# Building one triangular inverse of a chunked scan from the other by 32x32 block transposes, with the projection beside it in half-width units

## The reference, cut to what matters

```python
def wkv_scan(r, v, decay, k, a_in, b_in, s0, reverse):
    """S_t = S diag(w_t) + (S a_t) b_t^T + v_t k_t^T, y_t = S_t r_t."""
    def step(S, inp):
        rt, vt, wt, kt, at, bt = inp
        sa = jnp.einsum('bhij,bhj->bhi', S, at)
        S = S * wt[:, :, None, :] + sa[..., None] * bt[:, :, None, :] + vt[..., None] * kt[:, :, None, :]
        return S, jnp.einsum('bhij,bhj->bhi', S, rt)
    ...
for d in range(2):
    y_c, s_ctx_end = wkv_scan(r_c, v_c, *dirs_c[d], zeros, reverse=(d == 1))
    y_l, _ = wkv_scan(r_l, v_l, *dirs_l[d], s_ctx_end, reverse=(d == 1))
...
g_na, g_pool, g_rw = split(sigmoid(merge_logits))     # merge_logits = h @ w_in[:, last 6144 columns]
```

## Time and profile before

| what | value |
|---|---|
| time, three runs | 3787.69, 3774.82, 3781.83 us; median 3781.83 us |
| profiled execution, first to last instruction | 3780.2 us |
| instructions in it | 60072 |
| TensorE busy, share of the span | 3524.4 us, 93% |
| VectorE, ScalarE, GpSimd busy | 54%, 18%, 15% |
| mean granted TensorE clock | 0.982 of full speed |
| mean DMA rate | 211 GB/s |
| scan stage, from its first to its last visit on TensorE | 2799.4 to 3438.5 us, 639.1 us |

### The profile page before, as it was taken

One profiled execution on the slowest core, in us unless ns is written; L12 is line 12 of the kernel. 1 busy time (PEld: TensorE's weight loads), 2 busy tenths in 40 slices (PEclk: granted clock), 3 DMA queues, 4 the chain that ended last, 5 costly groups with the idle time before them and its releaser, 6 DMA issues. The chain is left out here.

```text
span 3780.2 us, 60072 instructions
## 1 busy us (share of the span) xinstructions
PE 3524.4 (93%) x24875; PEld 1824.6 (48%) x24875; DVE 2048.1 (54%) x3270; ACT 698.6 (18%) x1383; POOL 563.2 (15%) x809
## 2 busy tenths in 40 slices
PE   6999998999989998999999999989998899888998
PEld 2354443334544445554444444543356676665443
DVE  1699983352356776557646566436533334344435
ACT  2100001122210111431100000335622222221000
POOL 0111111120000002000000110631113223332100
PEclk9999999999999999999999999999999999999999
DMA  9989995982244467335477686558854333335663
GB/s 366 333 302 330 344 347 208 330 326 77 73 183 175 175 239 263 106 126 202 166 257 255 227 326 229 167 190 273 266 158 152 107 104 112 105 100 181 240 223 111
DMA packets 362625, 799.01 MB, mean 211 GB/s; under 512 B 26630, under 2 KB 73790, under 8 KB 357746
## 3 DMA queue, kind: packets, MB, share of 16 engines
q1 hardware_dynamic: 259760, 459.54, 35.5%
q0 software_dynamic: 72992, 274.20, 20.1%
q10 hardware_dynamic: 29602, 61.42, 4.3%
HBM read 686.90 MB, written 108.18 MB: 210 GB/s over the span
## 5 line engine op out<-in xcount | busy, mean ns | idle before, releaser
L1228 PE MATMUL gemm_a_g_ps<-store_w,turned 128*128 128x512 f32 (+1 forms) x1152 | 457.6, 560 | 2.7 <-PEq L108 2.7
L759 DVE SCALAR_TENSOR_TENSOR pmods_acc<-pmods_w,cond,pmods_acc 128x512 f32<-128x512 f32 x540 | 384.4, 749 | 23.6 <-issue 0.5
L1228 PEld LDWEIGHTS gemm_a_g_ps<-store_w,turned 128*128 128x128 f32 x1152 | 209.4, 191 | 250.3 <-issue 250.3
L3084 PE MATMUL scan_g_ps<-store_w,turned 64*64 64x512 f32 x2048 | 288.1, 610 | 10.5 <-DVE outlet_stage L3098 6.8
L1228 PE MATMUL att_a_g_ps<-store_w,turned 128*128 128x512 f32 x512 | 240.2, 599 | 6.9 <-ACT outlet_stage L2812 4.2
L1228 PE MATMUL feat_g_ps<-store_w,turned 128*128 128x512 f32 x384 | 181.9, 622 | 14.6 <-ACT outlet_stage L2240 12.4
L1275 PE MATMUL out_c_g_ps<-store_w,turned 128*128 128x512 f32 x384 | 167.6, 592 | 0.0
L1228 PE MATMUL tail_g_ps<-store_w,tail_branch_t 128*128 128x512 f32 x384 | 165.7, 592 | 0.9 <-ACT tail_branch_t L3913 0.9
L3449 DVE TENSOR_TENSOR scan_tm<-scan_tm,scan_ps 128x256 f32<-128x256 f32 x128 | 53.8, 421 | 168.8 <-PE scan_ps L3337 168.6
L1228 PEld LDWEIGHTS att_a_g_ps<-store_w,turned 128*128 128x128 f32 x512 | 91.5, 191 | 100.0 <-issue 93.4
L3337 PE MATMUL scan_ps<-scan_tmt,scan_y 64*64 64x64 f32 x2560 | 118.9, 223 | 14.2 <-issue 10.7
(11 more groups left out here) (577 smaller groups left out, 5934.0 us busy)
## 6 DMA issues: line engine op xcount, KB each, us to landing
store_w<-in_w_in SPq DMA_DIRECT2D x160, 1024.0 KB, 7.9
pmods_w<-in_w_mod POOLq DMA_DIRECT2D x40, 2048.0 KB, 13.2
store_w<-in_a_w_in SPq DMA_DIRECT2D x48, 1024.0 KB, 10.9
store_w<-in_c_w_in SPq DMA_DIRECT2D x40, 1024.0 KB, 8.4
first_mods_w<-in_w_mod SPq DMA_DIRECT2D x32, 1024.0 KB, 14.3
store_w<-in_a_w_out SPq DMA_DIRECT2D x32, 1024.0 KB, 6.2
scan_raw<-s_feat SPq DMA_DIRECT2D x112, 256.0 KB, 4.5
s_feat<-feat_o POOLq DMA_DIRECT2D x16, 1536.0 KB, 7.9
```

What stands on the lines that cost most here:

```text
L759: v.scalar_tensor_tensor(a, src, x, a, ALU.mult, ALU.add)
L1228: mm = pe.matmul(to, lhs, self.store.slot[i % self.store.NS][:, k, :width], start=first, stop=last)
L3084: mm = pe.matmul(self.ps[r][halves[o], :], self.act_tile(k, tb)[halves[r], halves[o]], self.store.slot[i % self.store.NS][halves[r], k % 4 ...
```

## The change

- TensorE: `products` no longer forms `A_`; `level(k)` makes only one product, with `y1` and `tmt`, on the diagonal quadrants, for all five levels.
- VectorE: `y1` is made here (`y_`), as the product of `half` plus the identity, in place of ScalarE's copy. The product of `level` is then the new `tmt` itself. `turn` makes `tm` from it by three block transposes (even heads: 128 partitions; odd heads: two of 64 partitions, each to the other half of the partitions), then a drain. A new stage `t0` adds the identity to the first `tmt` and turns it. `tm` is wanted only up to blocks of 32, so a transpose of 32x32 blocks is a whole one.
- ScalarE: `tt{k}` copies the product of `level` to `tmt`; for levels 1 to 4 it waits until VectorE has turned it.
- GpSimd: the two additions of the identity go.
- The projection: the 14 inner contraction steps of a tile are issued as two halves of 256 columns with a `yield` after each; the first and the last step stay whole and count as two units, of which one is empty for each. There are now 512 units, 40 ahead of the first visit, and the room is 6 behind `products`, 4 behind `av`, 1 behind each `half` and each `level`, 2 behind others.

```diff
 class Stream:
+    PER_TILE = 2 * KD
@@ units
-                for r, o in ((0, 0), (1, 1), (0, 1), (1, 0)):
-                    mm = pe.matmul(self.ps[r][halves[o], :], self.act_tile(k, tb)[halves[r], halves[o]],
-                                   self.store.slot[i % self.store.NS][halves[r], k % 4, :], start=(k == 0), stop=(k == KD - 1))
+                for ch in [slice(0, NCH)] if k in (0, KD - 1) else [slice(0, NCH // 2), slice(NCH // 2, NCH)]:
+                    for r, o in ((0, 0), (1, 1), (0, 1), (1, 0)):
+                        mm = pe.matmul(self.ps[r][halves[o], ch], self.act_tile(k, tb)[halves[r], halves[o]],
+                                       self.store.slot[i % self.store.NS][halves[r], k % 4, ch], start=(k == 0), stop=(k == KD - 1))
+                    if ch.start == 0:
+                        yield
@@ rwkv_scan
-        n_units, lead = len(gemm_side.tiles) * KD, 20
-        share = {"products": 6, "av": 3, "half": 1}
+        n_units, lead = len(gemm_side.tiles) * Stream.PER_TILE, 40
+        share = {"products": 6, "av": 4, "half": 1, "level": 1}
@@ products
                 inner(d, AT, 1, 0)
-                inner(d, A_, 0, 1, cross=True)
@@ half(k)
-                    if k > 1:
-                        after(pe, d, "dve", g, s, f"t{k - 1}")
-                    elif lat:
-                        after(pe, d, "dve", g, s, "rk")
+                    after(pe, d, "dve", g, s, "rk" if lat and k == 1 else f"t{k - 1}")
@@ level(k)
-                    after(pe, d, "act", g, s, f"half{k}")
-                    if k > 1:
-                        after(pe, d, "dve", g, s, f"tt{k - 1}")
-                    ...
+                    after(pe, d, "dve", g, s, f"y{k}")
+                    after(pe, d, "act", g, s, f"tt{k - 1}" if k > 1 else "av")
+                    for h in range(HG):
                         for c in chunks:
+                            mm = pe.matmul(quarter(d, 2, 1)[c, h, :], y1[d][c, h, :], tmt[d][c, h, :], start=True, stop=True)
@@ vector
-                v.tensor_tensor(by_parity(tm[d]), a, mask_by_parity(d, FIRST_T), ALU.mult)
+            def turn(d, src):
+                even, odd = by_parity(tm[d])[:, 0, :, :], by_parity(tm[d])[:, 1, :, :]
+                v.transpose(even, by_parity(src)[:, 0, :, :])
+                for c in range(2):
+                    v.transpose(odd[chunks[1 - c]], by_parity(src)[chunks[c], 1, :, :])
+                v.drain()
+                v.sem_inc(dve_done[d], 1)
+            def t0(d, g, s, lat):
+                v.tensor_tensor(tmt[d][:, :, :], tmt[d][:, :, :], eye, ALU.add)
+                v.drain()
+                turn(d, tmt[d][:, :, :])
+            def y_(k):
+                def f(d, g, s, lat):
+                    after(v, d, "pe", g, s, f"half{k}")
+                    v.tensor_tensor(by_parity(y1[d]), crossed(d, 0, 1), by_parity(eye), ALU.add).then_inc(dve_done[d], 1)
             def t_(k):
                 def f(d, g, s, lat):
                     after(v, d, "pe", g, s, f"level{k}")
-                    v.tensor_tensor(by_parity(tm[d]), by_parity(tm[d]), crossed(d, 0, 0), ALU.add).then_inc(dve_done[d], 1)
+                    turn(d, quarter(d, 2, 1))
-            def tt_(k):
-                ...
-                order = [("ft", 0), ("ft", 1), ("at", 0), ("ak", 0), ("at", 1), ("ak", 1)]
+                order = [("ft", 0), ("ft", 1), ("at", 0), ("ak", 0), ("at", 1), ("ak", 1), ("t0", 0), ("t0", 1)]
@@ scalar
-                run[f"half{k}"] = copies(f"half{k}", lambda d, lat, x: [(by_parity(y1[d]), crossed(d, 0, 1))])
+                run[f"tt{k}"] = copies(f"level{k}", lambda d, lat, x: [(tmt[d][:, :, :], quarter(d, 2, 1))], f"t{k}" if k < N_LEVELS else None)
@@ gpsimd
-                    pool.tensor_tensor(tm[d][:, :, :], tm[d][:, :, :], eye, ALU.add)
-                    pool.tensor_tensor(tmt[d][:, :, :], tmt[d][:, :, :], eye, ALU.add).then_inc(pool_done[d], 1)
```

More of the change, by code:

```diff
@@ L3065, in load_after @@
             old, part = (end - self.store.NS - begin) // 4, (end - self.store.NS - begin) % 4
-            if old >= 0 and 2 * KD * old + KD + 4 * (part + 1) > n_units:
+            if old >= 0 and self.PER_TILE * (2 * old + 1) + self.PER_TILE // 4 * (part + 1) > n_units:
                 break
@@ L3155, in stages @@
                 + ["tz", "outer", "chain1"] + ["y"] * lat + ["chain2"],
-                "dve": ["ft", "at", "ak"] + ["rk"] * lat + [f"{a}{k}" for k in levels for a in ("t", "tt")][:-2] + [f"tt{N_LEVELS}"] + ["pm", "m1", "m2"],
-                "act": ["ft", "av"] + [f"half{k}" for k in levels] + ["tz", "outer"] + ["y"] * lat,
-                "pool": ["eye"] + [f"lt{k}" for k in levels] + ["dg"],
+                "dve": ["ft", "at", "ak", "t0"] + ["rk"] * lat + [f"{a}{k}" for k in levels for a in ("y", "t")][:-1]
+                + ["pm", "m1", "m2"],
+                "act": ["ft", "av"] + [f"tt{k}" for k in levels] + ["tz", "outer"] + ["y"] * lat,
+                "pool": [f"lt{k}" for k in levels] + ["dg"],
             }[eng]
@@ L3265, in turned, with inner @@
                 mm.then_inc(pe_done[d], 1)
-            def inner(d, o, x, y, cross=False):
+            def inner(d, o, x, y):
                 for hp in range(0, HG, 2):
                     for h, to in ((hp, 0), (hp + 1, 1), (hp, 1), (hp + 1, 0)):
-                        c = 1 - to if cross and h % 2 else to
-                        mm = pe.matmul(product(d, o)[chunks[to], h % 2, h // 2, :], head(ft[d], h, x)[:, chunks[c]],
-                                       head(ft[d], h, y)[:, chunks[c]], start=True, stop=True)
+                        mm = pe.matmul(product(d, o)[chunks[to], h % 2, h // 2, :], head(ft[d], h, x)[:, chunks[to]],
+                                       head(ft[d], h, y)[:, chunks[to]], start=True, stop=True)
                 return mm
@@ L3352, in tz_ @@
             def tz_(d, g, s, lat):
-                after(pe, d, "dve", g, s, f"tt{N_LEVELS}")
+                after(pe, d, "act", g, s, f"tt{N_LEVELS}")
                 for h in range(HG):
@@ L3417, in _ @@
             v.wait_ge(tables, 64)
+            eye = eye2[:, :].unsqueeze(1).broadcast_to([P, HG, HD])
             def ft_(d, g, s, lat):
@@ L3448, in f @@
                     after(v, d, "pe", g, s, f"level{k}")
-                    v.tensor_tensor(by_parity(tm[d]), by_parity(tm[d]), crossed(d, 0, 0), ALU.add).then_inc(dve_done[d], 1)
-                return f
-            def tt_(k):
-                def f(d, g, s, lat):
-                    after(v, d, "pe", g, s, f"level{k}")
-                    v.tensor_tensor(tmt[d][:, :, :], tmt[d][:, :, :], quarter(d, 2, 1), ALU.add).then_inc(dve_done[d], 1)
+                    turn(d, quarter(d, 2, 1))
                 return f
@@ L3472, in m_ @@
                 return f
-            run = {"ft": ft_, "at": at_, "ak": ak, "rk": rk, "pm": pm_, "m1": m_(0), "m2": m_(1)}
+            run = {"ft": ft_, "at": at_, "ak": ak, "t0": t0, "rk": rk, "pm": pm_, "m1": m_(0), "m2": m_(1)}
             for k in levels:
-                run[f"t{k}"], run[f"tt{k}"] = t_(k), tt_(k)
-            made_by = {"ft": "turned", "at": "products", "ak": "products", "pm": "outer", "m1": "chain1", "m2": "chain2"}
-            made_by.update({f"{a}{k}": f"level{k}" for k in levels for a in ("t", "tt")})
+                run[f"y{k}"], run[f"t{k}"] = y_(k), t_(k)
+            made_by = {"ft": "turned", "at": "products", "ak": "products", "t0": "products", "pm": "outer", "m1": "chain1", "m2": "chain2"}
+            made_by.update({f"{a}{k}": f"{b}{k}" for k in levels for a, b in (("y", "half"), ("t", "level"))})
             t = 0
@@ L3486, in _ @@
                 names = stages("dve", steps[s][2])
-                order = [("ft", 0), ("ft", 1), ("at", 0), ("ak", 0), ("at", 1), ("ak", 1)]
-                order += [(stage, d) for stage in names[3:] for d in range(2)]
+                order = [("ft", 0), ("ft", 1), ("at", 0), ("ak", 0), ("at", 1), ("ak", 1), ("t0", 0), ("t0", 1)]
+                order += [(stage, d) for stage in names[4:] for d in range(2)]
                 for stage, d in order:
@@ L3498, in _, with copies @@
         def _(act):
-            def copies(name_of_product, pairs):
+            def copies(name_of_product, pairs, turned_first=None):
                 def f(d, g, s, lat):
                     after(act, d, "pe", g, s, name_of_product)
+                    if turned_first:
+                        after(act, d, "dve", g, s, turned_first)
                     for dst, src in pairs(d, lat, raw[s % 2][d]):
@@ L3527, in _ @@
                     for d in range(2):
-                        while t < tiles_by(max(0, visit_of[(g, s, "turned" if stage == "ft" else stage, d)] - 6)):
+                        while t < tiles_by(max(0, visit_of[(g, s, {"ft": "turned"}.get(stage, stage.replace("tt", "level")), d)] - 6)):
                             gemm_side.evict(act, t)
```

29 lines of the change are left out of this document (6 added, 23 removed).

## The result

The changed kernel takes 3806.73 us (median of 4 runs, 3802.07 to 3811.7) against 3783.61 us before (median of 4, with one more run beside it): ratio 1.0069, 95% interval 1.0054 to 1.0084. It is slower by 0.7%, where 0.5% faster was forecast, and lies just above the range of 3732 to 3800. The profiled execution is the slowest of the four (3811.7 us).

A forecast was written before the change was run, and what follows sets the result against it. TensorE, busy 93% of the span, was the starting bound; VectorE's turns would set the new level loop. Terms -19 + 7 - 11 + 5 = -18 us gave 3762, stated as 3763, range 3732 to 3800.

The forecast's parts named there:

- T: Duration of `turn`, three transposes on VectorE in each level's loop: taken as 0.80 us, bounds 0.68 and 1.07.
- rival (2): In `turn`, transposes stand end to end, T = 0.96: sum +2 us, 3784, no change; chance 0.22 shared with a lower-clock case.
- The levels: The 16 stretches from first `half` to `tz`: 15.77 us each against 16.96 before, 19 us won.
- The formula, 9.37 + 8T: Length in us of one stretch from first `half` to `tz`: four periods of 1.74 + 2T plus 2.41.
- The end of a tile: VectorE's endings of a projection tile, two operations in a queue with little slack in the levels: some 3 us lost.
- The half records: 1792 additional projection records from half-units: counted as nothing; 27 us if each cost its 15 ns.
- Late instructions: "issue" idle time of TensorE in the levels, 33.4 us: 11 taken as hidden, bounds none and 25.
- rival (1): In `turn`, transposes overlap like plain operations (T = 0.68), 25 us of late instructions absorbed: -50 us, 3732; chance 0.20.
- Work moved elsewhere: Outside the levels: 20.6 us of projection arrives, 8.0 of `A_` goes, units fill 6 of waits: net 7 us lost.
- The clock: TensorE's granted clock in the scan stage: more half-speed stretches, 2 us lost.
- the period as a function of T: Loop of one level over both directions: 1.74 + 2T us, set by VectorE and its turns, not TensorE.

The follow-up runs named there:

- e3: Changed kernel with VectorE ending a projection tile ahead of `t0` instead of behind it: 3797.6 us, ratio 1.0043 to the kernel before.
- e8: e3 plus a burst of units cut off where a tile ends, the rest coming behind the next pair of visits: 3788.8 us, ratio 1.0018 to before.
- e1: Changed kernel's new inverse alone, with the old whole units and old room: 3790.4 us, ratio 1.0025 to the kernel before.
- e7: Kernel before (old inverse) with contraction steps split into 256-column halves, units in their old places: 3810.6 us, ratio 1.0067 to before.
- e11: Uncrossed inverse with one transpose, tile ends ahead of `t0`, old places; against its whole-unit version (3737.7 us), inner steps split in halves: 3758.3 us.
- e10: e1 with each turn a single 128x256 transpose, `half` still reading as if crossed (wrong output, for time only): 3739.9 us, ratio 0.9888 to before.
- e6: Kernel before (old inverse) with the new unit places and room, but every contraction step issued whole: 3796.8 us, ratio 1.0040 to before.
- e4: Changed kernel with odd heads not crossed, one 128x256 transpose per turn, `half` on diagonal quadrants only: 3767.9 us, ratio 0.9962 to before.

## Why the prediction was wrong, step by step

**T, the step that took away the gain.** I took 0.80 us for `turn`, between three 128-element operations that overlap (0.68) and three of twice the elements (1.07). It measured 0.97. Each transpose by itself is 0.32, close to the row I had chosen (0.28), but none starts before the one ahead of it has ended, while the plain operations of my row start 0.20 us apart. Those all began in the same partitions; the transposes of a turn do not, and the copies at L2692 show that such a change alone keeps two operations apart. I had put the doubt on the transposing ("a turned block has to fill first") and had not looked at the partitions. T is that of rival (2), 0.96, whose sum gives 3784: by the formula 8 x 0.17 x 16 = 22 us more, which alone takes the sum from -18 to about +4 us.

**The levels.** The formula, 9.37 + 8T, gives 17.13 us, and the trace has 16.98 and 17.12 in two context rounds without "issue". But my base was high: 16.96 us is a mean with the half-speed pieces in it, and the kernel before has 16.27 and 16.53 in stretches without "issue". In all 16 stretches "issue" fell from 33.1 to 11.7 us, the waits for a tile's end rose from nothing to 2.9, and the sum fell by 9.7. So the rest of the levels, its work and its links, grew by about 9 us, where I had 19 less.

**The end of a tile, the step that made it a loss.** I priced VectorE's endings of a tile at 3 us, as a queue with less slack. They cost 26.1 - 5.2 = 21 us of idle TensorE, of which e3 and e8 gave back 18 in time. Two things were not seen: where tiles end within the new bursts, and that `t0`, which I had covered by the projection behind `products`, stands ahead of the sum in VectorE's list, for which that very projection waits. I asked what `t0` makes `half` wait for and not what is queued behind it.

**The half records.** I counted nothing for the 1792 additional records. In the changed kernel that comes out nearly right: e8 with half-units is at e1's time with whole ones, but for the order named there. In a kernel that TensorE bounds it is false: 29 us in e7, 21 in e11. That this is near the 27 us of the bound I had given is luck: the bound was 15 ns for each record, and in e7's clean stretch 50 more records cost 0.04 us. The price comes as "issue" and at a lower clock, in other stretches.

**Late instructions.** Of the 33.4 us in the levels I took 11 as hidden; 21 went, and 25 of 45.5 in the whole stage. The direction was right, the size near the bound given for rival (1).

**Work moved elsewhere.** Net 7 us; outside the levels 37 us were lost, about 18 of them in the tile's ends. The clock, 2 us in my sum, fell from 0.98 to 0.96 in the stage. By an estimate, 2% of some 560 us of work, that is 11 us, partly behind the long waits as at 2976. With +3 for the levels at T = 0.97, +7, -21, +21 and +11 the terms give about 21 us, where the medians have 23 and the profiled executions 30. I did not separate the remainder further.

**What held.** A level of 32 records at 0.86 to 0.90 us, a half-unit at 0.43, each hand-over of the loop, and the period as a function of T. That TensorE's own work would not set the period was right as well, and e10 shows it.

The page of the Trainium skill named in the prediction, "VectorE: DVE Perf Modes", says in "The DRAIN you can't avoid" that the next operation does not start until the pipe is empty, and also that one which is not held starts earlier; its "Rules for kernel authors" advise to keep the number of operations small. The trace has both: the transposes of a turn start 0.33 us apart for 0.32 each, the 128-element products 0.20 for 0.28. The same page's "The three transpose paths" has 311 ns for a 128x128 transpose in bf16; here one in fp32 takes 317 ns on average, so the trace agrees with that row to 2%, for another type.

## What to carry to other kernels

When an operation is new to an in-order engine, ask not only for its duration but whether the next one overlaps it, and look for any pair in the trace that moves between the same partitions: three short ones in a loop that two directions share count six times in a period. When units of filler work are cut finer, check three things apart: what they cover, how many more instructions they need, and where the boundaries that need another engine now fall. A use of all four quadrants that needs two more instructions on the engine in the loop can be worth less than half the array.

## What the runs showed of the hardware

- A block transpose of fp32 on VectorE takes 0.317 us for 128 partitions and 128 elements, 0.314 for 64 partitions and 128, and 0.450 for 128 and 256, out of PSUM: by the two with 128 partitions, some 0.18 us fixed and 1.04 ns an element of a partition. Three in a row that change the half of the partitions do not overlap.
- Two operations in a row on VectorE overlap by 0.08 to 0.09 us where they begin in the same partitions (0.28 us operations start 0.20 apart, the copies at 2384.51 and 2385.11). Where the second begins in the other half, it starts when the first has ended (two copies of 0.42 us in 0.85, eight times).
- "issue" idle time of TensorE goes with the number of records and with the slack between them: 63.1 us for 17596 records with little waiting, 45.5 for 15940 (33.4 in e6), 37.7 and 27.6 for 14780 in e4 and e11, 15.4 for 13124, 20.5 for 15036 where TensorE waits elsewhere for 64 us. So the number of records does not fix it alone. I read it as instructions that arrive late; the runs show the dependence, not the cause.
- After 7.1 us in which TensorE stood idle, the granted clock was 0.50 for the next 4.4 us, and its records took 4.32 us in place of 2.15.
- The same addition of the identity in SBUF (128x256, two inputs) took 0.42 to 0.46 us at 24 of its 32 times in the changed kernel and 0.81 at the other 8. I did not look for the reason.
